# Input tiles 5 to 15 of a hybrid decoder step: transposed by DMA from ScalarE's queue instead of by TensorE, with the order of all instructions chosen anew

## What is computed

```python
def rmsnorm(x, g):
    ms = jnp.mean(x * x, axis=-1, keepdims=True)
    return x * lax.rsqrt(ms + EPS) * g

u = rmsnorm(x, norm_g)                 # x: (2048, 1024) per core, and 16 sample rows
proj = u @ w_in                        # (2064, 8704)
lx, lg, sb, scg, sh, sg, q, qg, mg = jnp.split(proj, SPLIT_POINTS, axis=-1)
z_a = (rglru(causal_dwconv(lx)) * silu(lg)) @ lru_wo
z_b = (silu(sg) * sb * causal_dwconv(scg * sh)) @ sconv_wo
z_c = (attention(q, memory) * silu(qg)) @ xa_wo
g_a, g_b, g_c = jnp.split(sigmoid(mg), 3, axis=-1)
y = rmsnorm(x + (g_a * z_a + g_b * z_b + g_c * z_c) @ w_out, final_norm_g)
```

## Time and profile before

| | |
|---|---|
| median of 3 runs | 730.6 us (730.41 to 738.32) |
| profiled execution | 730.96 us on the device; span of the slowest core (core 7) 729.6 us |
| PE busy | 711.8 us (98% of the span) |
| DVE, ACT, POOL busy | 406.1, 346.7, 174.1 us (56%, 48%, 24%) |
| chain that ended last | PE 92%, DMA 5% |
| PE's transposes (L827) | 152, first at 10.3 us, last at 71.1 us |

### The profile page before, as it was taken

The page is one execution under the profiler, slowest core; times in us unless marked ns, Lnnn a source line. Parts: engine busy times, 40 slices in busy tenths (PEclk is TensorE's granted clock), DMA queues, the critical chain, the costliest instruction groups (busy, mean ns, idle before and its releaser), DMA issues.

```text
span 729.6 us, 13649 instructions; the slowest of 8 cores (725.9 to 729.6 us)
## 1 busy us (share of the span) xinstructions
PE 711.8 (98%) x5177; PEld 472.7 (65%) x5177; DVE 406.1 (56%) x418; ACT 346.7 (48%) x459; POOL 174.1 (24%) x213
## 2 busy tenths in 40 slices
PE   6999999999999999999999999999999999999996
PEld 5977676666666566666666666666666666665442
DVE  2455243958649669697486898932032222215667
ACT  2556469779496897853952322121211121121445
POOL 4444100000000010000100433652226363144000
PEclk8899999999999999999999999999999999999999
DMA  8994932121112211122233666763225769055745
GB/s 186 252 222 117 149 91 44 18 40 32 30 30 35 39 30 30 30 32 38 37 69 75 133 134 168 152 96 49 36 37 80 94 80 163 2 174 180 222 179 219
DMA packets 29487, 69.78 MB, mean 96 GB/s; under 512 B 3456, under 2 KB 7872, under 8 KB 29168
## 3 DMA queue, kind: packets, MB, share of 16 engines
q0 software_dynamic: 18000, 31.60, 29.5%
q1 hardware_dynamic: 11424, 37.32, 15.7%
HBM read 90.73 MB, written 9.88 MB: 138 GB/s over the span
## 4 chain that ended last, share of the span: by engine, by line
PE 92%; DMA 5%; issue 1%; DVE 1%; POOL 1%; ACT 1%; POOLq 0%; DVEq 0%; ACTq 0%
PE PP L732 72%; PE PP L1327 8%; PE PP L776 7%; DMA R<-w_in 2%; PE PP L1086 2%; DMA R<-xa_wo 2%; PE PP L827 1%; PE PP L1078 1%; PE PP L1014 1%; DMA R<-cv 1%; POOL R L140 1%; DVE R L830 0%; ACT R L935 0%; PE PP L1205 0%; DVE R L819 0%
## 5 line engine op out<-in xcount | busy, mean ns | idle before, releaser
L732 PE MATMUL PP<-R 128*128 128x344 bf16 x3768 | 557.9, 309 | 1.3 <-ACT R L935 0.5
L732 PEld LDWEIGHTS PP<-R 128*128 128x128 bf16 x3768 | 366.9, 98 | 187.0 <-issue 5.8
L1263 ACT ACTIVATE R<-PP 128x688 f32<-128x688 f32 x72 | 53.3, 743 | 196.0 <-PE PP L732 179.6
L1272 DVE SCALAR_TENSOR_TENSOR R<-R,PP 128x688 f32<-128x688 f32 x72 | 62.2, 869 | 124.0 <-PE PP L732 122.0
L140 POOL DMA_DIRECT2D R<-w_in x68 | 38.7, 570 | 284.8 <-PE PP L732 235.7
L776 PE MATMUL PP<-R 128*128 128x128 bf16 (+3 forms) x672 | 58.1, 245 | 5.1 <-DMA R<-w_in 2.9
L776 PEld LDWEIGHTS PP<-R 128*128 128x128 bf16 x672 | 48.0, 102 | 12.8 <-issue 6.1
L1327 PE MATMUL PP<-R 128*128 128x512 bf16 x256 | 55.7, 379 | 0.0
L1276 POOL TENSOR_TENSOR R<-R 128x688 f32<-128x688 f32 x24 | 40.3, 1687 | 48.5 <-DVE R L1272 48.1
L1281 POOL TENSOR_TENSOR R<-R 128x688 bf16<-128x688 f32 x24 | 40.7, 1701 | 31.8 <-DVE R L1272 27.7
L1327 PEld LDWEIGHTS PP<-R 128*128 128x128 bf16 x256 | 25.0, 98 | 29.8 <-issue 0.2
(11 more groups left out here) (137 smaller groups left out, 563.6 us busy)
## 6 DMA issues: line engine op xcount, KB each, us to landing
R<-w_in POOLq DMA_DIRECT2D x68, 256.0 KB, 4.4
R<-xp SPq DMA_DIRECT2D x32, 512.0 KB, 9.8
R<-ck SPq DMA_DIRECT2D x16, 512.0 KB, 4.4
y_p<-R SPq DMA_DIRECT2D x15, 512.0 KB, 2.8
R<-cv POOLq DMA_DIRECT2D x16, 256.0 KB, 7.7
R<-w_out POOLq DMA_DIRECT2D x8, 256.0 KB, 10.1
R<-xa_wo POOLq DMA_DIRECT2D x14, 128.0 KB, 5.4
R<-sconv_wo POOLq DMA_DIRECT2D x8, 192.0 KB, 3.8
```

Source lines behind the costliest of these rows:

```text
L732: return lambda e: e.matmul(ps.ap[:, b * 512:b * 512 + BLK], lhs(k), rhs[:, k, c:c + BLK], start=(k == 0), stop=(k == nk - 1))
L1263: G.act(lambda e, ps=pg[u], th_=th_: e.activation(out=b3(th_.ap), in_=pv(ps), func=AF.Tanh, scale=0.5), UW, [pg[u].tok], [th_.tok], Px - E ...
L1272: G.dve(lambda e, zp=zp, th_=th_, dst=dst: e.scalar_tensor_tensor(out=b3(dst.ap), in0=b3(th_.ap), scalar=1.0, in1=pv(zp), op0=ALU.add, op1 ...
```

## The change

1. For tiles 5 to 15 (`TURN`) PE's eight transposes and DVE's eviction from PSUM are gone. DVE now scales the tile by the row's power and, in the same instruction, by the norm weight (L831 of the changed kernel). Then one transfer per tile, issued from ACT's queue, reads the 128 x 8 x 128 bf16 values from SBUF and writes them transposed into `uT` (DMA_TRANSPOSE, L142). Each has a semaphore of its own (`turn5` to `turn15`).
2. The norm weight is now needed along the row, on all partitions: a transfer of 512 KB, `gbx`, copies the vector `norm_g1` to 128 partitions.
3. Tiles 0 to 4, the sample tile and the two memory tiles go as before.
4. `SHIFT` has new numbers throughout, so the order is another one on every engine and in the whole program.

```diff
+TURN = range(5, 16)
@@ Sched.dma
             for out, in_ in pairs:
-                eng.dma_start(out=out, in_=in_).then_inc(sems[semkey], 16)
+                if turn:
+                    eng.dma_start(out=out, in_=in_, transpose=True).then_inc(sems[semkey], 16)
+                else:
+                    eng.dma_start(out=out, in_=in_).then_inc(sems[semkey], 16)
@@ SHIFT
-    "first2.pool": 0.5, "x0.pool": -40, "x0.dve": -1.5, "x1.act": -87.5, "x1.pool": 9, "x1.pe": -18, "x1.dve": -26, "x2.act": 84.5,
...
+    ".pool": -36, ".pe": 3.5, "x0.act": -16, "x0.pool": -41.5, "x0.dve": 36, "x0.pe": 110.5, "x1.act": -66.5, "x1.dve": 39.5,
...
@@ Graph.run
             if t.dma is not None:
                 q = t.eng
-                if start < 58.0:
+                if q == "act":
+                    dmafree[q] = end + 2.5
+                elif start < 58.0:
...
@@ build_program
+    norm_g1 = din("norm_g1", [D])
...
+        m_gbx = Mem("gbx", m_xc.off, 1024, F32)
+        gbx = m_gbx.ap
...
@@ p0
             rstd(ti, nr, prio)
+            if ti in TURN:
+                G.dve(lambda e: e.scalar_tensor_tensor(out=xn_.ap, in0=x_.ap[:, 0:1024], scalar=stat[:, ti:ti + 1], in1=gbx,
+                                                       op0=ALU.mult, op1=ALU.mult), 1024, [x_.tok, t_st[ti], m_gbx.t], [xn_.tok], prio)
+                G.dma("act", [(dst, lambda: xn_.ap.rearrange("p (k d) -> p k d", k=KC))], 262144, [xn_.tok], [tdst], prio, f"turn{ti}", turn=True)
+                t_tr.append(G.tasks[-1])
+                return x_.tok
...
+            if i == 3:
+                G.tag = "gbx"
+                G.dma("sp", [(gbx, norm_g1.partition_broadcast(128))], 524288, [], [m_gbx.t], -96.5, "gbx")
```

More of the change, by code:

```diff
@@ L128, in op, with dma @@
         self._done((key, st.cnt), reads, writes)
-    def dma(self, key, semkey, pairs, reads, writes, stores):
+    def dma(self, key, semkey, pairs, reads, writes, stores, turn=False):
         st = self.streams[key]
@@ L216 @@
 class Task:
-    __slots__ = ("i", "eng", "dur", "fns", "reads", "writes", "prio", "hs", "tset", "npred", "succ", "pf", "dma", "preds", "start", "gate", "etset", "xgate", "stores", "key")
+    __slots__ = ("i", "eng", "dur", "fns", "reads", "writes", "prio", "hs", "tset", "npred", "succ", "pf", "dma", "preds", "start", "gate", "etset", "xgate", "stores", "key", "turn")
 SHIFT = {
[13 rows of a table removed]
-    "kv.pool": -6.5, "kv.act": -47, "kv.sp": -30.5, "kv.dve": -128.5, "gates0.pe": -40.5, "gates0.act": 19.5, "rec0.act": 66.5,
[54 rows of a table removed]
[66 rows of a table added]
 }
@@ L384, in pool, with dma @@
         return self._add("pool", dur, [fn], reads, writes, prio)
-    def dma(self, q, pairs, nbytes, reads, writes, prio, sem, stores=False):
+    def dma(self, q, pairs, nbytes, reads, writes, prio, sem, stores=False, turn=False):
         t = self._add(q, (0.65 if q == "pool" else 0.45) * len(pairs), None, reads, writes, prio, dma=(pairs, nbytes, sem))
         t.stores = stores
+        t.turn = turn
         return t
@@ L422, in run @@
         busy = dict.fromkeys(free, 0.0)
-        dmafree = {"pool": 0.0, "sp": 0.0}
+        dmafree = {"pool": 0.0, "sp": 0.0, "act": 0.0}
         curset = None
@@ L495, in run @@
                 q = t.eng
-                if start < 58.0:
+                if q == "act":
+                    dmafree[q] = end + 2.5
+                elif start < 58.0:
                     dmafree[q] = max(dmafree[q], end + (2.9 if q == "pool" else 0.8)) + t.dma[1] / 155e3
                 else:
-                    f = max(dmafree.values())
-                    dmafree = dict.fromkeys(dmafree, max(f, end + 0.8) + t.dma[1] / 280e3)
+                    f = max(dmafree["pool"], dmafree["sp"])
+                    dmafree["pool"] = dmafree["sp"] = (max(f, end + 0.8) + t.dma[1] / 280e3)
                 fin = dmafree[q] + 2.0
@@ L523, in run @@
                     sem = h.ring.sem + str(h.phys)
-                S.dma(t.eng, sem, [(o() if callable(o) else o, i() if callable(i) else i) for o, i in pairs], reads, writes, t.stores)
+                S.dma(t.eng, sem, [(o() if callable(o) else o, i() if callable(i) else i) for o, i in pairs], reads, writes, t.stores, t.turn)
             else:
@@ L804, in build_program @@
         t_rs, t_tr, t_xd = [], [], []
+        m_gbx = Mem("gbx", m_xc.off, 1024, F32)
+        gbx = m_gbx.ap
+        for k in ["gbx"] + [f"turn{i}" for i in TURN]:
+            dsem(k)
         def rstd(col, nr, prio):
@@ L1452 @@
         "lru_wo": rows(lru_wo[0], 128), "sconv_wo": rows(sconv_wo[0], 128), "xa_wk": rows(xa_wk[0], XW)[0],
-        "xa_wv": rows(xa_wv[0], XW)[0], "xa_wo": rows(xa_wo[0], 128), "w_out": f(w_out[0]), "final_norm_g": f(final_norm_g),
+        "xa_wv": rows(xa_wv[0], XW)[0], "xa_wo": rows(xa_wo[0], 128), "w_out": f(w_out[0]), "final_norm_g": f(final_norm_g), "norm_g1": f(norm_g[0]),
     }
```

## The result

The changed kernel takes 759.71 us (median; 757.84 to 760.57) where the kernel before took 730.5 beside it: 1.0381 times as long, 95% interval 1.0335 to 1.0427. It is slower by 29.2 us; the forecast was 731.9, and the range ended at 744. The profiled execution lasted 760.47 us, its span on the slowest core (4) is 758.9. An execution in which the cores of one half of the chip ran at a lower granted clock than the others (in e10_mid one of 863 us, at 0.82 to 0.85) is left out of the ratios and of e10_mid's time.

What follows compares the result with a forecast made beforehand. The prediction took PE's list of work, busy 711.8 of 729.6 us, to set the end. Its terms, -4.9 + 1.4 + 1.7 + 2.6 + 0.5, gave +1.3 us and a forecast of 731.9 us, range 725.5 to 744.

Steps and rivals of the forecast that it cites:

- what is taken away: On PE's list, eleven sets of eight transposes go at 0.45 us each: -4.9 us; DVE's changes counted as nothing.
- The first turned tile: PE asks for tile 5 at 36.1 us, its transfer lands at 37.8: +1.7 us (0 to 6.6).
- The later tiles: PE asks for tile 10 at 54.6 us, it is turned at 57.2: +2.6 us (0 to 6), nothing more from tile 11.
- ACT's own time: Eleven issues on ACT's queue at 0.41 us, 4.5 us in all, fit in its idle time: nothing on the path.
- Rival C: Issues of 1.86 us each hold ACT, evictions come late and PE waits for PSUM: about 738 us, chance 0.17.
- The rest of the order: New order in the whole program, PE's waits between 100 and 690 us: counted 0, with 2.5 us either way.
- The load ahead of the first tile: The 512 KB load first on SP's queue puts every x tile one place later: +1.4 us (0.45 to 3.7).
- The tail: After the last matmul, PE's list ends with whole tile 14, not tile 15 in halves: +0.5 us (0 to 1.2).
- A: Rival: turned tiles go one at a time on ACT's queue, each taking long: about 750 or 805 us, chance 0.12.
- The estimate of 10.5 us a tile: Argument against the change: a turned tile's eight blocks, by DMA one after another at 1309 ns each, take 10.5 us.

Runs made afterwards that it cites:

- e10_mid: e9_back with one w_in load moved ahead of two adds on POOL and six x loads made to wait for one xa_wo load: +9.5 us, ratio 1.0128.
- e9_back: The changed kernel in its new order, with PE transposes and a DVE eviction where ACT issued each transfer: +16.0 us, ratio 1.0222 to the kernel before.
- e5_tiny: The changed kernel with each of the eleven transfers cut to an ordinary one of 32 bytes, output not the reference's: +10.3 us, ratio 1.0141.
- e2_long: The changed kernel with the transfers as ordinary copies to contiguous places, in 2 KB packets, output not the reference's: +14.9 us, ratio 1.0205.
- e6_tiny_gbx: e5_tiny with the 512 KB load moved from first place on SP's queue to behind x tile 4: +10.8 us, ratio 1.0148.
- e11_head: e9_back with PE's first groups put back in the old sequence: +13.3 us, ratio 1.0182 to the kernel before.
- e8_oldorder: The kernel before in its old order, with tiles 5 to 15 turned by transfers issued where PE's transposes stood: +30.7 us, ratio 1.0424.
- e1_plain: The changed kernel with the transfers as ordinary copies into the same small pieces, output not the reference's: +24.9 us, ratio 1.0342.

## Why the prediction was wrong, step by step

**The sign came from two terms of the sum.** The prediction counted 1.7 + 2.6 for the turned tiles and 1.4 + 0.5 + 0 for head, tail and order. The runs give the order with its head and tail 16.0 in place of 1.9 (e9_back; some 4 of it may belong to the places where that run puts the transposes). They give the transfers 18.9 in place of 4.3 (the changed kernel against e5_tiny: 29.2 - 10.3). Only the term for what is taken away was right: -4.9. With half of PE's work at half clock taken off (11.7 of 23.4 us in the changed kernel, 3.8 of 7.6 before), PE's list is 703.0 us in place of 708.0.

**The first turned tile: the landing was mis-sized.** The step itself was right up to the issue. Tile 4's transposes began at 29.96 (prediction 29.4), PE asked for tile 5 at 36.8 (36.1), and the transfer was issued at 33.17 (32.4). Then the time from issue to landing was taken as 5.4 us, with 10.3 as the upper bound, and it was 18.1. Both bounds came from rows whose transfers go in packets of 2 and 4 KB, and the 5.4 from a stretch in which SP's and POOL's queues took 22.8% and 43.9% of the engines (88 to 100 us); the number of packets was not in the argument. The runs divide the 18.1: 7.4 for a transfer of hardly any bytes on these engines, 10.6 with 128 packets of 2 KB for the tile, 18.4 with 1024 small ones, and nothing more of landing for turning. The old trace held the hint: a w_in load of the same 256 KB took 10.3 there, so 5.4, chosen because the queue was new and empty, had to be too low. An empty queue didn't help, because the engines behind it were full.

How the packets take turns is seen in the changed kernel's queues (packets, MB, share), from 41 to 45 us and, when the loads ran out, from 48 to 51:

```profile
q1 hardware_dynamic: 223, 0.82, 65.1%
q0 software_dynamic: 161, 0.27, 38.4%
q10 hardware_dynamic: 218, 0.06, 6.5%
```
```profile
q10 hardware_dynamic: 886, 0.22, 114.0%
q1 hardware_dynamic: 75, 0.25, 20.2%
```

From 33 to 38 us, for nearly 5 us behind the issue, ACT's queue moved no packet; in e5_tiny it was the same (4.8 of the 7.4 us). From 41 to 45 it got 218 packets, SP's 223: nearly one for one, 0.06 MB against 0.82. In e2_long, with packets of 2 KB, from 42 to 46 us:

```profile
q0 software_dynamic: 176, 0.32, 43.4%
q1 hardware_dynamic: 173, 0.63, 42.7%
q10 hardware_dynamic: 172, 0.31, 20.9%
```

As many turns, and over five times the bytes. The Trainium skill, page DMA: Bandwidth & Descriptors, section Queues, rings and completion order, says that an engine goes round its queues packet by packet. The traces agree by these counts (218 to 223, 172 to 173 to 176); POOL's queue, with 161 beside 218, got less, and whether the profile's packet is the page's no run shows. This was the rule against the change, and the prediction didn't have it.

**The later tiles.** Tile 10 was not the one that came late. Tile 8 did (2.3 us): by the chain its transfer, issued at 60.01, stood on ACT behind evictions of work that PE did only after tile 5 had landed, and it took 7.5 us. So did tile 11 (4.4 us), whose 13.8 us ran beside the memory tiles' loads at 67 to 77 us, where the prediction counted the engines as free. Measured 6.7 for 2.6.

**ACT's own time.** 0.41 us an issue was taken from SP's rows; a transposing issue took 1.25 us at the least and 12.54 at the most. Rival C had that price (1.86) but not the mechanism: a second issue can last while the transfer ahead of it is under way (12.54 us, to 3.5 us before tile 5 landed).

**The rest of the order.** "It can win that at most there, and it can lose as much": the second half has no ground. Waits of 2.5 us in the old order bound what a new one can win; they say nothing on what it can lose. Two loads that came 2 to 2.5 us late were worth 6.5 us.

**The load ahead of the first tile.** 29.96 for 29.4 looks like a hit, but the cause was another: moving the load changed nothing (e6_tiny_gbx against e5_tiny), PE's sequence of groups did (e11_head). The first x tile landed at 8.73 (near 10 forecast). Right by its number, wrong by its reason.

**The tail.** 2.0 for 0.5. From PE's end to the last power's end it was 3.4 us (3.2 forecast); but from the end of the two halves (754.91) to the end of the span passed 4.0 us where 2.8 was counted.

**What no term held: the clock.** On the slowest core the three waits for turned tiles and one of 2.1 us for xa_wo each brought a stretch at half clock behind them, 8 us in all, so that PE's list didn't shrink by 4.9 but grew by 2.9. A wait as long needn't do so: on core 2 of the same execution one of 2.0 us, at 450.5, left the clock at 1.00.

**The rivals.** A came nearest, with a chance of 0.12: its lower figure was 750, and a landing of 10.3 us for each was too little for tile 5 and too much for tiles 14 and 15 (3.1). The estimate of 10.5 us a tile that stood there beside the Trainium skill's page VectorE: DVE Perf Modes (The three transpose paths) doesn't hold where the engines are free: 3.1. The Trainium skill's page Advanced Engine Details and Errata, section X-Bar Transpose (TRN2), on which such transfers are as fast as ordinary ones, agrees with the trace as to landing, 18.1 to 18.4, but not as to the engines' time, 33.8% to 18.6% (last section). It decided nothing: the ordinary copy was as slow.

## What to carry to other kernels

Price a transfer by its packets and by what else the engines carry when it is issued, and not by its bytes or by whether its own queue is empty; here a thousand small packets landed when the large ones of the other queues had nearly gone. A trace in which PE hardly waits bounds what a new order can win, never what it can lose, so an order chosen anew is a term with a wide bound of its own, and each new wait of PE may cost again in half clock behind it. Measure such a change in halves, the moved work in the old order and the new order without the moved work, and don't expect the halves to add up: here they were 30.7 and 16.0 for a whole of 29.2.

## What the runs showed of the hardware

- Beside full queues a transfer of 32 bytes took 7.4 us from issue to landing, where the engines were free 1.65; one of 256 KB in 1056 small packets took 18.1 and 3.1. The second of these is in the issues of the changed kernel from 84 to 99 us (tiles 14 and 15; median us to landing last):

```profile
R<-R ACTq DMA_TRANSPOSE x2, 3.1
```

- A second transposing issue on ACT's queue lasted 12.54 us (14.1 in e8_oldorder) while the first transfer was under way. An ordinary issue of the same tile lasted 0.60.
- Transposing packets took longer on the engines than ordinary ones of the same size: 2.88 MB took 33.8% of the engines' time from 30 to 100 us in the changed kernel and 18.6% in e1_plain, and as 2 KB packets 11.2%.
